# Layer 1's windowed attention worked by head pairs, with row halves for the scores and column halves for the weighted sums

## What is computed

```python
def _gqa_attend(q, k, v, sink, mask):            # 4 query heads share a key head
    s = einsum('bqhgd,bkhd->bhgqk', qg, k) / sqrt(d)
    s = where(mask, s, NEG_INF)
    p = softmax(concatenate([s, sk], axis=-1), axis=-1)[..., :-1]    # sk: the sink
    o = einsum('bhgqk,bkhd->bqhgd', p, v)

def _swa_mixer(...):
    # a block of 128 queries sees the 256 context keys and the blocks before, at and after it,
    # where |key - query| <= 128 and the key exists
    y = swapaxes(lax.map(block, ...)).reshape(b, s, -1) @ w_o
```

## Time and profile before

| | us |
|---|---|
| median of 3 runs | 3292.8 (3288.74 to 3293.56) |
| the profiled execution's own time | 3286.71 |
| its span in the trace | 3284.8 |
| layer 1's attention, from its first score matmul to the next phase | 185.2 |

### The profile page before, as it was taken

One profiled execution on the slowest core, in us unless ns is written; L12 is line 12 of the kernel. 1 busy time (PEld: TensorE's weight loads), 2 busy tenths in 40 slices (PEclk: granted clock), 3 DMA queues, 4 the chain that ended last, 5 costly groups with the idle time before them and its releaser, 6 DMA issues. The chain is left out here.

```text
span 3284.8 us, 31063 instructions
## 1 busy us (share of the span) xinstructions
PE 2677.5 (82%) x12000; PEld 1404.0 (43%) x12000; DVE 1057.7 (32%) x2331; ACT 545.7 (17%) x1184; POOL 190.4 (6%) x281
## 2 busy tenths in 40 slices
PE   8959998869487777748898587777669587899999
PEld 1124445645353333324685354433334354344444
DVE  1122217766422222246443422222145444110000
ACT  0000104432010000012442000000012353100000
POOL 0010000000011111100000011111100100000000
PEclk9979999989699999979999699999989798899999
DMA  9831000020499999841002599999750101322110
GB/s 327 306 135 51 26 2 1 1 99 26 177 413 416 416 416 416 367 165 39 17 1 92 202 414 415 416 415 416 297 193 13 45 1 64 128 77 76 66 64 26
DMA packets 161658, 594.46 MB, mean 181 GB/s; under 512 B 20896, under 2 KB 23456, under 8 KB 128740
## 3 DMA queue, kind: packets, MB, share of 16 engines
q1 hardware_dynamic: 150952, 571.45, 44.3%
q0 software_dynamic: 10560, 21.01, 1.7%
HBM read 581.81 MB, written 24.22 MB: 184 GB/s over the span
## 5 line engine op out<-in xcount | busy, mean ns | idle before, releaser
L1506 PE MATMUL moe_down<-moe_wd,moe_hid_t 128*64 128x512 f32 x1024 | 243.8, 619 | 78.4 <-DMA moe_wd<-in_moe_w_down 70.4
L1480 PE MATMUL moe_up<-moe_wu,moe_xg_t 128*64 128x256 f32 x2048 | 238.3, 386 | 72.5 <-DMA moe_wu<-in_moe_w_up 72.5
L1480 PE MATMUL moe_gate<-moe_wg,moe_xg_t 128*64 128x256 f32 x2048 | 238.6, 386 | 62.1 <-DMA moe_wg<-in_moe_w_gate 60.5
L451 PE MATMUL qkv_acc<-qkv_w,a_buffer 128*128 128x512 f32 x576 | 253.4, 596 | 9.1 <-DMA qkv_w<-in_a_w_qkv 9.1
L2406 PE MATMUL mlp_acc<-m_h,mlp_w 128*128 128x512 f32 x512 | 224.2, 599 | 11.3 <-DMA mlp_w<-in_w_up 9.3
L1480 PEld LDWEIGHTS moe_gate<-moe_wg,moe_xg_t 128*64 128x64 f32 x2048 | 149.8, 139 | 174.2 <-DMA moe_wg<-in_moe_w_gate 105.4
L2421 PE MATMUL mlp_acc<-mlp_w,mlp_u_t 128*128 128x512 f32 x512 | 220.0, 592 | 1.4 <-DVE mlp_u_t L2441 1.4
L1480 PEld LDWEIGHTS moe_up<-moe_wu,moe_xg_t 128*64 128x64 f32 x2048 | 148.0, 138 | 160.8 <-DMA moe_wu<-in_moe_w_up 97.0
L1086 PE MATMUL out_acc<-out_w,out_o_t 128*128 128x512 f32 x448 | 205.2, 618 | 6.8 <-ACT out_o_t L934 3.5
L293 PE MATMUL mod_acc<-mod_w,mod_act 128*2 128x512 f32 x384 | 167.9, 600 | 14.3 <-DMA mod_w<-in_mod_w 14.3
L451 PEld LDWEIGHTS qkv_acc<-qkv_w,a_buffer 128*128 128x128 f32 x576 | 108.3, 192 | 136.4 <-issue 127.0
(11 more groups left out here) (367 smaller groups left out, 3035.6 us busy)
## 6 DMA issues: line engine op xcount, KB each, us to landing
moe_wg<-in_moe_w_gate SPq DMA_DIRECT2D x64, 2048.0 KB, 28.0
moe_wu<-in_moe_w_up SPq DMA_DIRECT2D x64, 2048.0 KB, 28.3
moe_wd<-in_moe_w_down SPq DMA_DIRECT2D x64, 2048.0 KB, 28.1
mod_w<-in_mod_w SPq DMA_DIRECT2D x24, 2048.0 KB, 8.8
mlp_w<-in_w_up SPq DMA_DIRECT2D x8, 2048.0 KB, 8.8
mlp_w<-in_w_down SPq DMA_DIRECT2D x8, 2048.0 KB, 7.8
qkv_w<-in_a_w_qkv SPq DMA_DIRECT2D x6, 2048.0 KB, 8.2
in_w<-in_w_in SPq DMA_DIRECT2D x4, 2048.0 KB, 17.9
```

What stands on the lines that cost most here:

```text
L451: mm = nc.tensor.matmul(acc[i % 4][:], h_t[:, k, t * P:(t + 1) * P], w[:, b % ring, k, :], start=(k == 0), stop=(k == KD - 1))
L1480: mm = nc.tensor.matmul(acc[b][halves[f], 0:HF], xg_t[b][:, k, c, :], w[b][:, c, k, f * HF:(f + 1) * HF], start=(c, k) == (0, 0), stop=(c, ...
L1506: mm = nc.tensor.matmul(down[b][halves[c], :], hid_t[:, k, h, :], wd[b][:, 2 * h + k, c * NCHUNK:(c + 1) * NCHUNK], start=(k, h) == (0, 0) ...
```

## The change

One function, `window_attention`, takes the place of the 64 units. It works on 32 groups g, each a query block b and a pair of heads c (blocks in the order 0, 3, 1, 2). q is scaled by -0.125, the mask is +1e30 and the sinks are negated, so that VectorE's minimum gives the negated maximum at once. The sink is one more column of the exponential's input. The probabilities are divided by their sum before they are transposed. `k_t` has a single version; head m of a pair uses rows 64m to 64m+63 of q and k. The weighted sum has the values as weights (64 columns) and the probabilities streaming, into partitions 64m to 64m+63. The output is feature-major, so layer 1's `project_out` doesn't transpose it.

```diff
+def window_attention(nc, e, q_t, k_t, v, o_t):
+    order = [(b, c) for b in (0, 3, 1, 2) for c in range(8)]
...
+        masked = ph.sb("masked", [P, 2, 2, 641])
+        prob = ph.sb("prob", [P, 3, 2, 641])
+        score = [ph.ps(f"score{i}", [P, 1024]) for i in range(2)]
+        tp = [ph.ps(f"tp{i}", [P, 4, P]) for i in range(2)]
+        out = [ph.ps(f"out{i}", [P, 4, P]) for i in range(2)]
...
+            def scores(g):
+                b, c = order[g]
+                if g >= 1:
+                    pe.wait_ge(s["masked"], 2 * g)
+                runs = key_runs(b)
+                for col, token, w in runs:
+                    for m, rows in enumerate(HALVES):
+                        mm = nc.tensor.matmul(score[m][:, col:col + w],
+                                              q_t[rows, c, b * P:(b + 1) * P],
+                                              k_t[rows, c // 2, token:token + w],
+                                              start=True, stop=True)
+                        if (col, token, w) == runs[-1]:
+                            mm.then_inc(s["scored"], 1)
+            def turn(g, j):
+                if j == 0:
+                    pe.wait_ge(s["scaled"], 2 * g + 2)
...
+                if z >= 2:
+                    pe.wait_ge(s["read_t"], z - 1)
...
+            def weigh(g):
...
+                pe.wait_ge(s["read_t"], first[g + 1])
+                for k, t in enumerate(tiles_of(b)):
+                    for m, rows in enumerate(HALVES):
+                        mm = nc.tensor.matmul(out[g // 4 % 2][rows, g % 4, :],
+                                              v[:, t, c // 2 * HD:(c // 2 + 1) * HD],
+                                              prob_t[:, g % 2, m * kt(g) + k, :], start=(k == 0),
+                                              stop=(k == kt(g) - 1))
+                mm.then_inc(s["weighed"], 1)
+            scores(0)
+            scores(1)
+            for g in range(n + 1):
+                if g < n:
+                    turn(g, 0)
+                    turn(g, 1)
+                if g >= 1:
+                    weigh(g - 1)
+                if g < n and len(batches[g]) > 2:
+                    turn(g, 2)
+                if g + 2 < n:
+                    scores(g + 2)
...
+            def mask_and_max(g):
...
+                for m in range(2):
+                    dve.wait_ge(s["scored"], 2 * g + m + 1)
+                    if g >= 2:
+                        dve.wait_ge(s["exped"], 2 * (g - 2) + m + 1)
+                    nc.vector.tensor_tensor_reduce(
+                        masked[:, g % 2, m, 0:width], score[m][:, 0:width], masks[:, b, 0:width], 1.0,
+                        sinks[:, 2 * c + m:2 * c + m + 1], ALU.add, ALU.min,
+                        neg_top[:, g % 2, m:m + 1]).then_inc(s["masked"], 1)
+                    if m == 0:
+                        v_.tensor_copy(masked[:, g % 2, :, width], sinks[:, 2 * c:2 * c + 2]).then_inc(
+                            s["sunk"], 1)
+            def scale(g):
+                width = kt(g) * P
+                dve.wait_ge(s["exped"], 2 * g + 2)
+                link(v_.reciprocal(inv[:], total[:, g % 3, :]))
+                for m in range(2):
+                    x = prob[:, g % 3, m, 0:width]
+                    v_.tensor_scalar(x, x, inv[:, m:m + 1], None, ALU.mult).then_inc(s["scaled"], 1)
...
+            mask_and_max(0)
+            for g in range(n + 2):
+                if g + 1 < n:
+                    mask_and_max(g + 1)
+                if g < n:
+                    scale(g)
+                if g >= 5 and (g - 5) % 4 == 0:
+                    read_out((g - 5) // 4)
...
+            for g in range(n):
+                read_t(g, 0)
+                read_t(g, 1)
+                if len(batches[g]) > 2 and g + 2 >= n:
+                    read_t(g, 2)
+                if g + 2 < n:
+                    exponential(g + 2)
+                    if len(batches[g]) > 2:
+                        read_t(g, 2)
```

A batch of `turn` is four transposes into one of two PSUM banks; `read_t` is ScalarE's copy of a batch. A group of four key tiles has two batches, one of five tiles has a third of two transposes. In `project_out` (without a gain) and `enter_layer_1`:

```diff
-            turn_o(0)
+            if gain is not None:
+                turn_o(0)
             for i in range(nt + 1):
                 if i < nt:
                     products(i)
-                if i + 1 < nt:
+                if i + 1 < nt and gain is not None:
                     turn_o(i + 1)
...
-        @block.gpsimd
-        def _(pool):
-            for half in range(2):
-                nc.gpsimd.memset(k_t[HALVES[1 - half], half], 0.0).then_inc(s["zeroed"], 1)
...
-                    for half, rows in enumerate(HALVES):
-                        nc.scalar.copy(k_t[rows, half, :, t * P:(t + 1) * P],
-                                       tp[j % 2][rows]).then_inc(s["tp_read"], 1)
+                    nc.scalar.copy(k_t[:, :, t * P:(t + 1) * P], tp[j % 2][:]).then_inc(
+                        s["tp_read"], 1)
```

More of the change, by code:

```diff
@@ L72, in constants @@
         k = np.arange(max(0, b - 1) * P, min(TX, b + 2) * P)[None, :]
-        band[b, :, CTX:CTX + k.shape[1]] = np.where(np.abs(k - b * P - q) <= 128, 0, NEG)
+        band[b, :, CTX:CTX + k.shape[1]] = np.where(np.abs(k - b * P - q) <= 128, 0, -NEG)
     out["band"] = band
@@ L847, in project_out @@
         w = ph.sb("w", [P, 2, KD, NCHUNK])
-        o_t = ph.sb("o_t", [P, 2, KD, P])
+        o_t = None if gain is None else ph.sb("o_t", [P, 2, KD, P])
         gates = ph.sb("gates", [P, 2, D])
@@ L957, in square_and_root @@
                                      bias=eps[:]).then_inc(s["n_std_done"], 1)
[L959 to L965, removed]
+            if gain is not None:
+                square_slices(0)
+                root_slices(0)
+                square_slices(1)
+                copy_o(0)
+                root_slices(1)
+                square_slices(2)
+                root_slices(2)
             for i in range(nt + 1):
-                if i + 1 < nt:
+                if i + 1 < nt and gain is not None:
                     copy_o(i + 1)
@@ L1065, in turn_o @@
             def turn_o(i):
-                if gain is not None:
-                    pe.wait_ge(s["o_done"], i + 1)
+                pe.wait_ge(s["o_done"], i + 1)
                 for half in range(2):
@@ L1077, in products @@
             def products(i):
-                pe.wait_ge(s["tp_read"], 2 * i + 2)
+                if gain is not None:
+                    pe.wait_ge(s["tp_read"], 2 * i + 2)
+                lhs = (lambda k: o[:, k, i * P:(i + 1) * P]) if gain is None else (
+                    lambda k: o_t[:, i % 2, k, :])
                 for c in range(2):
@@ L1085, in products @@
                             pe.wait_ge(loaded[2 * c + k // 4], 16)
-                        mm = nc.tensor.matmul(acc[j % 3][:], o_t[:, i % 2, k, :], w[:, c, k, :],
+                        mm = nc.tensor.matmul(acc[j % 3][:], lhs(k), w[:, c, k, :],
                                               start=(k == 0), stop=(k == KD - 1))
@@ L1639, in enter_layer_1 @@
     side = lambda t: 0 if t >= TC else 1
-    reads = [0]
-    for _, c in items:
-        reads.append(reads[-1] + (2 if c == 2 else 1))
     with Phase(nc, "qkv1") as ph:
@@ L1657, in enter_layer_1 @@
         names = ("gates_in vec_in rope_in y_in combined sq_done summed std_done eps_done h_done n_tp_done "
-                 "n_tp_read mm_done acc_read tp_done tp_read zeroed step")
+                 "n_tp_read mm_done acc_read tp_done tp_read step")
         s = {x: ph.sem(x) for x in names.split()}
@@ L1826, in turn_heads_of @@
                 if j >= 2:
[L1827 removed]
+                    pe.wait_ge(s["tp_read"], j - 1)
                 for q in range(4):
@@ L1862, in layer_1 @@
         h_t = buffer[:].rearrange("p (k n) -> p k n", k=KD)
-        o = buffer[:, 0:TX * D].rearrange("p (t d) -> p t d", t=TX)
-        with sb("b_q", [P, 8, SEQ], F32) as q_t, sb("b_k", [P, 2, 4, NT * P], F32) as k_t, \
+        o = buffer[:, 0:TX * D].rearrange("p (k n) -> p k n", k=KD)
+        with sb("b_q", [P, 8, SEQ], F32) as q_t, sb("b_k", [P, 4, NT * P], F32) as k_t, \
                 sb("b_v", [P, NT, 4 * HD], F32) as v:
             enter_layer_1(nc, e, last_r, h_t, q_t, k_t, v)
[L1867 to L1891, removed]
+            window_attention(nc, e, q_t, k_t, v, o)
         project_out(nc, e, "out1", o, stream, None, None, 1.0, e["b_w_o"][0], mod_part(e, 1, 2),
```

84 lines of the change are left out of this document (82 added, 2 removed).

## The result

The changed kernel takes 3362.04 us, the median of 4 runs (3361.59 to 3362.82), against 3290.77 (3287.85 to 3293.56, 4 runs on the same chip). The ratio is 1.0217, with a 95% interval of 1.0199 to 1.0235. The forecast of 3361 came true.

The account below looks back on a forecast made before the run. TensorE was taken as hardly ever idle in the attention, but after the change a closed ring sets the time: 231 + 27 = 258 us against 185.2, +72.8, less 4.1, +68.7. Forecast 3361 us, range 3305 to 3405.

Parts of the forecast that it names:

- the ring: Attention: masks, division, transposes, sums and scores wait for one another in a closed round; 7.56 (four tiles 6.37) us a turn.
- the lower clock: Attention: TensorE's waits of about 3 us lower its granted clock; one turn in two loses 1.7 us, 27 us in all.
- The open ring: Rival: TensorE issues the next group's scores while VectorE divides; turns of 3.9 us on average, kernel 3242; chance 0.07.
- The turn at full clock: Attention: one group's share of the period, priced from profile rows at 7.56 us for five tiles and 6.37 for four.
- Sums: Attention, TensorE: 20 (16) records of weighted sums at 0.06 us, 1.20 (0.96) a turn; upper end 0.12 each.
- Changes: TensorE switching between whole array and halves: 0.14 us each, four (three) a turn, 0.56 (0.42); ends 0 and 0.14.
- Scores until the first mask: Attention: from the scores' issue until VectorE can mask, both heads side by side on row halves; 1.40 (1.19) us a turn.
- The start: Beginning of the attention: wait for the mask, negated sinks, first masks and second group's scores add 10.7 us.
- The rival of full clock throughout: Attention: TensorE's unbroken 4 us per turn keeps the clock up; 27 us less, kernel 3334, or 3318 without change costs; chance 0.19.
- ScalarE at no cost: Attention: ScalarE's exponentials and copies lie beside the ring and cost nothing; without that cover 1 us a turn.
- Projection out: Projection out loses its transposes and ScalarE's copies: 1.77 us before tile 1, 0.88 each before tiles 2 and 3; -3.5 us.
- The key copy: The last key copy is one instead of two in 1.18 us: -0.6 us.

Follow-up runs that it names:

- opening the ring: Against the changed kernel, TensorE issues the scores of group g+2 before the transposes of g instead of behind the third batch; 3231.04 us.
- the run with six changes: Against the kernel with scores issued first, the second batch of transposes stands between two parts of the sums; 3238.63 us.
- the wait filled: Against the changed kernel, TensorE does one unused matmul of 256 columns per key tile before each group's first transposes; 3317.07 us.

## Why the prediction was right

The forecast named the ring, where it closes, and the lower clock, and the runs bear out all three. Its total is right within 1 us, but that is luck in part: two terms were off by 15 and 18 us in opposite directions.

**The ring.** Right. The waits are those forecast (2.98 us before the transposes, 3.35 before the masks), opening the ring takes 131 us away, and a shorter division is worth 28 us inside and nothing outside. The open ring was priced at 3.9 us a turn and 3242; it came to 3.5 and 3231.

**The turn at full clock** was sized 0.5 us too long: 7.06 instead of 7.56, and 5.86 instead of 6.37. By its parts:

- Masks: 0.88 from start to start for five tiles and 0.74 for four, where I had 0.92 and 0.80. The earlier trace rows have no mask behind a mask, and I had read them up to the negation.
- The sink's copy: nothing, where 0.15 was charged. It is issued at 1712.60 and the second mask starts at 1712.68, beside it. The negation of the earlier trace rows reads the mask's own result; this copy doesn't. That was the wrong row to price it by.
- Divisions: 1.02 for two instead of 1.11. One lasts 0.55, as interpolated, but the second starts 0.47 after the first.
- Sums: 1.07 us for 20 records, 0.053 each instead of 0.06. The upper end, 0.12, is out. By the Trainium skill's "TensorE: Matmul & The Clock Gate", Part 3, loads run beside matmuls only where the row group differs. The trace disagrees with that rule: here all use the same 128 rows, and each load lasts 0.13 to 0.14 us while two matmuls start every 0.109.
- Changes: 0.17 us of load gap three times in a turn; the fourth lies under the wait for the division. I had 4 x 0.14. The price itself, 0.15 by the run with six changes, agrees with the earlier trace rows. It also puts a number on the drain that the Trainium skill names in "TensorEngine Tiling (Array Packing)", Tiling Modes.
- Scores until the first mask: 1.48 instead of 1.40. Row halves side by side was the right choice. The two heads' last records start 0.007 us apart, so the first mask waits for both heads in effect.
- The start: turns began at 1572.33, 10.3 us after the first score, for 10.7.

So the phase at nearly full clock (0.98, with the wait filled) takes 216.3 us and not 231.

**The clock.** The mechanism was right, the share wrong. The step that failed is "one turn in two to lose 1.7 us": 27 us, where 45 were lost. All but three of the 31 turns had a clock under 1.00 for part of them, most at 0.61 to 0.80. One long wait in the experts said what one wait costs, but not how often a wait that comes back every 7 us does it. The same rows warned of this: a wait of 2.45 us has 32 records in 3.67 us behind it, so it cost nothing, while the shorter one of 1.94 cost 1.7. And I misread: the 2 us with 0.25 us of records are that wait itself, and before it stood 3.67 us without a break. The upper end, every turn, 54, was the nearer one. The rival of full clock throughout had 3334; with the wait filled the kernel took 3317, 17 less, which is the oversized turn again.

**ScalarE at no cost.** Right at this size of turn, and the cover is thin. With 0.65 us less on VectorE, a wait of 0.42 for ScalarE's copy took most of it back.

**Projection out.** 2.9 us less from the first product to the last router product (76.9, against 79.8), for a forecast of 3.5. All three transposes that were priced are gone, and all that isn't product fell by 3.7 us. The clock moved the products both ways: those of the first two tiles take 29.0 us instead of 29.8, those of the last 15.7 instead of 14.0. TensorE's timeline has them in its last row, 1.7 us above those of the tile before:

```profile
1829.82 29.12 PE L1280 MATMUL out_acc<-out_w,b_buffer 128*128 128x512 f32 x64 [7.11 <-DMA out_w<-in_b_w_o]
...
1862.41 13.98 PE L1280 MATMUL out_acc<-out_w,b_buffer 128*128 128x512 f32 x32
...
1879.86 15.68 PE L1280 MATMUL out_acc<-out_w,b_buffer 128*128 128x512 f32 x32
```

The transposes were hidden under the weights' transfer for tile 0, as forecast, but this transfer then landed 0.7 us later after the phase's start than before (6.0 instead of 5.3). Why is open.

**The key copy.** The 0.6 us aren't to be seen: the first score starts at 1562.04, 0.5 later than before, in one execution each. In the experiments it started between 1563 and 1566 with the same work ahead of it, so a term of this size can't be read from a single execution.

**The sum.** The attention: +76.5 us instead of +72.8, that is 15 less at full clock and 18 more for the clock. Projection out and the copy: -1.7 (less 2.9, more 0.7 for the weights and 0.5 ahead of the first score) instead of -4.1. The remaining 1.3 of the 76.1 lies in other phases, in one execution each.

## What to carry to other kernels

Halving the work of the busiest engine is worth what the written order lets through: follow one buffer from its read to its next write over all engines, and if each engine's stretch on that round waits for the one before, the period is their sum, whatever the shares of busy time say. Look then for the instruction that can be issued earlier, because its inputs have long been there; here it was two lines, and they made the slower kernel (3362) one that beats both (3231). And price the clock for every period and not for some: where TensorE waited some 3 us in each turn of 7, all but three of 31 turns ran in part at the lower level, at a mean of 0.76.

## What the runs showed of the hardware

- Work added to TensorE made the kernel 45 us faster: 144 matmuls whose result nobody uses, in waits of 3 us, took the granted clock of the phase from 0.76 to 0.98.
- Records for the other half of the array don't wait for their place in the program. In these runs they start beside the fourth record from the end of the first half (with four per head 0.013 us behind the first, with six 0.006 behind the third, with ten 0.006 behind the seventh), in row halves and in column halves alike. Here, issuing two halves' records in turn was needed only where each half had more than four in a row.
- A change between the whole array and halves costs 0.15 us of TensorE, in the mean of the two directions, and is seen as a gap of 0.17 us in its loads; between column halves and row halves the gap is the same. Where TensorE waits anyway it costs nothing that shows: in the ring the first transpose starts at 1714.75, 0.06 us after the divisions' end.
